# Two-block transformer stack, one core: openings that take three weight units by operand tile, and the norm's sum inside the fourth

## The reference, cut to what matters

```python
x = x + rms_norm(merged @ w_out[i], norm_mix_post[i])
h = rms_norm(x, norm_ffn_pre[i])
ff = (jax.nn.silu(h @ w_ffn_gate[i]) * (h @ w_ffn_up[i])) @ w_ffn_down[i]
x = x + rms_norm(ff, norm_ffn_post[i])
e = (p[i] @ w_ple_proj[i]) * jax.nn.sigmoid(x @ w_ple_gate[i])
x = x + rms_norm(e, norm_ple[i])
```

## Time and profile before

| what | value |
|---|---|
| median of the runs | 2955.51 us |
| the profiled execution | 2956.12 us, of which its span is 2954.2 us |
| PE busy | 2911.0 us, 99% of the span |
| PE's granted clock over the span | 0.997 |
| ACT, DVE, POOL busy | 1288.0, 1262.4, 1429.0 us |
| DMA | 273.36 MB, mean 93 GB/s |

### The profile page before, as it was taken

How to read it: one execution, slowest core, us unless ns; L and a number is a source line. 1 busy time by engine, 2 the same in 40 slices (tenths; PEclk the granted TensorE clock), 3 DMA queues, 4 the chain that set the end, 5 groups by cost and what they waited for, 6 DMA issues and landing times.

```text
span 2954.2 us, 40036 instructions
## 1 busy us (share of the span) xinstructions
PE 2911.0 (99%) x14264; PEld 2386.1 (81%) x14264; DVE 1262.4 (43%) x2116; ACT 1288.0 (44%) x2011; POOL 1429.0 (48%) x811
## 2 busy tenths in 40 slices
PE   8999999999989999999999989999999999999999
PEld 7878887888878878887888877778888887888887
DVE  5546434221053656434222075654555128455510
ACT  4556545222243556444223255554444238444421
POOL 4665555444445755555444444344444442444443
PEclk9999999999999999999999999999999999999999
DMA  4222232333322222333333322112333322223332
GB/s 144 73 86 79 82 123 89 95 96 100 107 86 87 72 93 65 93 121 98 99 92 106 103 77 79 58 51 93 99 93 99 98 95 93 93 94 98 97 106 89
DMA packets 77274, 273.36 MB, mean 93 GB/s; under 512 B 8776, under 2 KB 9416, under 8 KB 77152
## 3 DMA queue, kind: packets, MB, share of 16 engines
q1 hardware_dynamic: 74112, 266.05, 28.8%
q10 hardware_dynamic: 3040, 5.64, 0.6%
HBM read 269.55 MB, written 2.10 MB: 92 GB/s over the span
## 4 chain that ended last, share of the span: by engine, by line
PE 93%; DVE 3%; ACT 1%; POOL 1%; issue 1%; DMA 0%; SPq 0%; DVEq 0%; ACTq 0%; POOLq 0%
PE ps L809 26%; PE ps L811 25%; PE ps L810 25%; PE ps L1090 2%; PE ps L1121 2%; PE ps L1068 2%; PE ps L1346 2%; PE ps L1352 1%; PE ps L1347 1%; PE ps L1194 1%; PE ps L1200 1%; PE ps L1195 1%; PE ps L1063 1%; POOL WLO L2802 1%; PE ps L881 0%
## 5 line engine op out<-in xcount | busy, mean ns | idle before, releaser
L2802 POOL TENSOR_TENSOR WLO<-WRAW,WHI 128x1024 fp32r<-128x1024 f32 x441 | 1064.3, 2417 | 1188.0 <-ACT WHI L1504 1187.9
L809 PE MATMUL ps<-HH,WHI 128*128 128x512 f32 x2184 | 857.1, 392 | 1.2 <-POOL WLO L2802 0.9
L811 PE MATMUL ps<-HH,WLO 128*128 128x512 f32 x2184 | 850.3, 389 | 0.0
L810 PE MATMUL ps<-HL,WHI 128*128 128x512 f32 x2184 | 850.0, 389 | 0.0
L1504 ACT ACTIVATE WHI<-WRAW 128x1024 fp32r<-128x1024 f32 x467 | 490.6, 1051 | 282.1 <-DMA WRAW<-wall 281.5
L809 PEld LDWEIGHTS ps<-HH,WHI 128*128 128x128 f32 x2184 | 410.1, 188 | 89.0 <-issue 4.8
L811 PEld LDWEIGHTS ps<-HH,WLO 128*128 128x128 f32 x2184 | 410.0, 188 | 86.2
L810 PEld LDWEIGHTS ps<-HL,WHI 128*128 128x128 f32 x2184 | 410.3, 188 | 82.9
L2654 DVE SCALAR_TENSOR_TENSOR ps<-U,COLS,ps 128x512 f32<-128x512 f32 x192 | 145.1, 756 | 120.9 <-ACT ps L1941 106.8
L2160 DVE TENSOR_TENSOR ACC<-ACC,SQ 128x512 f32<-128x512 f32 x80 | 70.5, 881 | 285.7 <-ACT SQ L1782 271.1
L809 PE MATMUL ps<-F2H,WHI 128*128 128x512 f32 x384 | 149.4, 389 | 0.0
(11 more groups left out here) (407 smaller groups left out, 4730.6 us busy)
## 6 DMA issues: line engine op xcount, KB each, us to landing
WRAW<-wall SPq DMA_DIRECT2D x502, 512.0 KB, 3.5
y<-X ACTq DMA_DIRECT2D x8, 256.0 KB, 3.8
X<-xin SPq DMA_DIRECT2D x3, 512.0 KB, 7.6
DFT<-dft ACTq DMA_DIRECT2D x4, 258.0 KB, 4.2
PT_IN<-pin ACTq DMA_DIRECT2D x2, 512.0 KB, 3.7
DIL<-dil ACTq DMA_DIRECT2D x1, 768.0 KB, 4.3
X<-xin SPq DMA_DIRECT2D x2, 256.0 KB, 4.5
COLS<-cols ACTq DMA_DIRECT2D x1, 290.5 KB, 5.3
```

The lines of the kernel that those rows point to most:

```text
L809: pe.matmul(out_, WHI[w_at], x_hi, start=first, stop=False)
L810: pe.matmul(out_, WHI[w_at], x_lo, start=False, stop=False)
L811: return pe.matmul(out_, WLO[w_at], x_hi, start=False, stop=last)
L2802: pool.tensor_tensor(WLO[:, s, :], whole, WHI[:, s, :].bitcast(F32), ALU.subtract).then_inc(wt_lo, 1)
```

## The change

The loop over tiles takes units 0, 1 and 2 alike: six matmuls by `high` and three by `low` for each tile. The lagging unit and its constant are gone. The wait for unit 2's low half and bank stands ahead of the first tile instead of ahead of the fourth. The norm's sum moves from between units 2 and 3 into unit 3, behind its third tile, and the spread moves from behind unit 3's fourth tile to behind its sixth. No matmul, weight or bank is added or removed.

```diff
-LAG = 3
+SUM_AT, SPREAD_AT = 3, 6
...
             def opening_slow(st):
-                for j in range(2):
+                for j in range(3):
                     opened(st, j)
-                for i in range(DT + LAG):
+                for i in range(DT + 1):
                     if i < DT:
                         pe.wait_ge(S["operand_hi_ready"], st.op_hi + i + 1)
-                        for j in range(2):
+                        for j in range(3):
                             high(st, j, i)
-                    if 1 <= i <= DT:
+                    if i:
                         pe.wait_ge(S["operand_ready"], st.op + i)
-                        for j in range(2):
+                        for j in range(3):
                             mm = low(st, j, i - 1)
                             if i == DT:
                                 mm.then_inc(unit_used, 1)
-                    if i == LAG:
-                        opened(st, 2)
-                    if i >= LAG:
-                        mm = part(st, 2, 2, pair["H"], i - LAG, i == LAG, i == DT + LAG - 1)
-                mm.then_inc(unit_used, 1)
-                if st.norm is not None:
-                    norm_sum(st.norm)
                 opened(st, 3)
                 for i in range(DT):
-                    if i == DT // 2 and st.norm is not None:
+                    if i == SUM_AT and st.norm is not None:
+                        norm_sum(st.norm)
+                    if i == SPREAD_AT and st.norm is not None:
                         norm_spread(st.norm)
                     mm = part(st, 3, 3, pair["H"], i, i == 0, i == DT - 1)
                 mm.then_inc(unit_used, 1)
```

## The result

The changed kernel takes 2967.78 us (median of six runs, 2966.48 to 2969.92) against 2955.51 us, a ratio of 1.0042 with an interval of 1.0031 to 1.0052. It is 12.3 us slower where 3.7 us were forecast, and lies above the range. Its profiled execution has a span of 2967.9 us and took 2969.92 us. Lines 1218 and up of the kernel before stand five lines higher in it, so L2802 is L2797, L2151 is L2146 and L2299 is L2294.

A forecast was written before the change was run, and what follows sets the result against it. The PE's chain, 93% of the span, was taken as the bound. Two swiglu openings at -0.1, two ple at +1.7 and proj 1 at +0.5 gave +3.7 us on 2955.5, so 2959.2 us, range 2955.8 to 2962.5.

The forecast's parts named there:

- The view that bounds the kernel: Whole kernel: the last-ending chain runs through the PE for 93% of the span, so only its issue times count.
- The later start: Swiglu and ple openings: PE waits for unit 2's low half, starting 1.3 and 1.4 us later, with 0.06 us signal.
- The clock: Rival at four swiglu and ple openings: longer idle lowers PE clock, 4.8 us each, 2964.0 to 2978 us; chance 0.06.
- a sign of being wrong: The forecast is wrong if the clock falls at an opening, ple's unit 4 shows no wait, or spread awaits factors.
- The rival's price per fall: At an opening with low clock: 24 matmuls run instead of 45, 21 times 0.226, 4.8 us; chance 0.06.
- The release of unit 4: Unit 0's slot is released 1.81 us later relative to the opening's end; 1.6 us of idle in ple.
- Swiglu's second wait: Ahead of swiglu's unit 4: DVE's scaling frees its bank at 484.71, a little after the low half; swiglu gains 0.1 us.
- The spread: In unit 3: about 3.0 us behind the sum; factors ready 2.25 us after the sum's start, wait hidden by 0.7 us.
- Proj 1: Its opening has no PE idle to give and ends unchanged; unit 4 starts 0.5 us later.
- The sum: Whole kernel: two swiglu openings at -0.1, two ple at +1.7, proj 1 at +0.5, together +3.7 us.
- The loads: Rival at unit 4: three loads share their time, each chain up to 1.7 us longer, 2967.7 us; chance 0.05.

The follow-up runs named there:

- the run with four fillers: Changed kernel plus four small matmuls of constants behind unit 0's wait ahead of the swiglu and ple openings; 2961.91 us.
- the run with the wait alone: Kernel before, lag of three tiles kept, only the wait for unit 2's low half hoisted ahead of the first tile; 2961.65 us.
- both runs with filled norms: Constants' matmuls around the norms ahead of proj 1 and qkv: on the kernel before, 2954.88 us; on the changed kernel with idle and release mended, 2947.07 us.

## Why the prediction was wrong

- **The view that bounds the kernel** was right: only the PE's order and idle counted.
- **The later start.** 1.3 and 1.4 us were worked out; the idle grew by 1.58 us in swiglu 0 and 1.65 in ple 0, since from POOL's end to the first matmul it took 0.36 us and not 0.06. That is 0.3 us in each of four openings. With the constants' matmuls between unit 0's wait and the other two it took 0.21 us in seven of eight openings; what sets this time stays open.
- **The clock** is the step that failed. The sum put its fall at nothing; as a rival it had 0.06, with the argument that after 2.90 us of idle the clock was still at full when the sums began, so 2.7 us would be harmless. It fell at all four openings, which the prediction itself had named as a sign of being wrong, and that cost some 8.0 us. The row doesn't show what was read from it, because the fall can come late: in the run with four fillers it came when the PE had been at work again for 1.2 us, and in the kernel before at 880.33, 1.70 us behind the first sum. In the run with the wait alone the same idle ahead of the same norm took the clock down before the sums began (windows of the kernel before; then timeline and window of the wait alone):

```profile
878.65:880.33 1.68, 1.01 (x8) 0.92 (x8) 0.16 (x1) 0.06 (x1) 0.39 (x1) 1.00 0.05 17
880.33:881.00 0.67, 0.00 (x1) 0.00 (x1) 0.00 (x0) 0.00 (x0) 0.67 (x2) 0.50 0.00 0
...
880.48 1.84 PE L836 MATMUL ps<-ONES,ACC 128*128 128x1 f32 x8 [2.89 <-DVE ACC L2158]
...
879.95:880.48 0.53, 0.00 (x0) 0.03 (x1) 0.39 (x1) 0.53 (x1) 0.00 (x0) 0.50 1.05 433
```

  So the first of proj 1's three idle times is enough by itself to take the clock down. At about 2.9 us of idle the clock fell in 11 of the 12 openings of the three kernels that had it, at 1.9 to 2.0 us in 3 of 4. The page "TensorE: Matmul & The Clock Gate" of the Trainium skill, section "Why this matters for your kernels", warns against idle gaps between bursts of matmuls, but the gaps that it names are somewhat longer than these, so the rival's sum doesn't follow from it, though the prediction says so. In kind the traces agree with it, in length they don't, and the measurement decides. The rival's price per fall, 4.8 us, was too high, since the low stretches lasted 3.41 or 6.83 us and not 10.24.
- **The release of unit 4.** The mechanism held, and the size nearly: 1.6 us of idle were forecast in ple, and it is 1.25 and 1.42 us.
- **Swiglu's second wait.** DVE's scaling releases unit 4, not WLO, as worked out, with 0.20 us of idle.
- **The spread** found its factors ready, as said.
- **Proj 1** was to lose 0.5 us. Its unit 4 does come late, 0.52 us behind the matmul before it where 0.23 is the usual distance. But the stretch from its norm to the next gained 1.0 us: its low clock lasted 6.83 us here and 10.24 us before, which none of its own rows foretold.
- **The sum.** With the clock kept up by filler, the changed kernel is 4.4 us slower than before; the sum had 3.7. Counted as in the table above, its stages lose 0.0 and 0.2 us in swiglu (forecast -0.1) and 2.1 and 1.9 us in ple (forecast +1.7). The loads didn't hold each other up: no wait ahead of unit 4 was longer than forecast.

## What to carry to other kernels

A wait that is moved ahead of the first matmul of a stage is paid twice: once for its own length, and once for what the PE's clock does after the longer idle. The second price is seen only behind the wait, in the clock of the next few microseconds, and mending one idle can bring up the next one further on. Put the wait behind the first real work, or make what is waited for earlier on an engine that idles, and only then count what the new order gives. When several buffers are finished together, the refill of the first one comes late: finish one of them early, and read the slack of its chain to the next use.

## What the runs showed of the hardware

- The granted clock fell at 11 of 12 openings behind 2.9 us of idle, at 3 of 4 behind 1.9 to 2.0 us, and at none of 28 behind 1.3 to 1.4 us. The same 2.9 us took it down in one opening and not in its twin.
- Behind 1.33 and 1.27 us of idle and then eight matmuls of one column it fell in both runs with filled norms, 1.50 us after these matmuls began. So 1.3 us of idle isn't harmless at every place.
- The fall has no fixed place behind the idle: in the changed kernel's swiglu 0 it came at 460.53, during the idle, in the run with four fillers 1.2 us after the PE had resumed. Full clock at the first matmuls is no sign that the idle was harmless. The low stretches lasted 3.41, 6.83, 10.24 or 13.65 us. In one kernel and another the same place had different lengths, and the difference alone is worth 1 to 2 us a place.
- Small matmuls of constants in place of the idle, 2.84 us of them ahead of the four openings, held the clock up. With 1.05 us of them and 1.9 to 2.0 us of idle behind, it fell in three of four.
- A low half of 128 x 1024 ahead of these openings took 1.23 us on DVE and 2.4 us on POOL.
